# A hybrid layer on one core: the first two weight slots cut finer, two queues for the first loads, and the last product's banks seeded earlier

## The chip, the cores and the metric

The kernel runs on one core of one Trainium2 chip. Its time is the device time of one execution in microseconds. Three runs of the kernel before gave a median of 928.58 us (928.54 to 929.57). The profile is one further execution with its own time of 928.34 us; its span, from the first to the last recorded instruction, is 926.5 us.

TensorE is called PE here, VectorE DVE, ScalarE ACT, GpSimd POOL, and SP is the engine that issues most of the DMAs.

## The reference

One layer over 512 tokens of width 1024, float32: a norm, a mixer of three branches (retention, sliding-window attention, a gated linear recurrence) with sigmoid gates, a cross-attention into 256 memory tokens, and a gated ConvFFN, each added to the residual, and a last norm.

```python
for l in range(DEPTH):                     # DEPTH = 1
    h = rms_norm(x, norm_mix_g[l])
    x = x + hybrid_mixer(h, w_in[l], swa_sinks[l], lb_all[l], hg_norm_g[l], w_branch[l],
                         w_out[l], cos, sin)
    h = rms_norm(x, norm_mem_g[l])
    x = x + mem_xattn(h, rms_norm(mem, mem_norm_g[l]), w_mq[l], w_mkv[l], w_mo[l])
    h = rms_norm(x, norm_ffn_g[l])
    ...
```

`rms_norm` multiplies a token by `rsqrt(mean(x * x) + EPS)` and by a gain per channel. The mixer's first product is `h @ w_in`, cut by columns into the inputs of the branches. The last product is `(silu(a) * u) @ w_down`; behind it stand the residual sum and the last norm.

## The kernel before

**Precision.** Every large product is done in three matmuls of a rounded format: an upper part and a lower part of each operand, as upper x upper, upper x lower, lower x upper. For activations these are `hH` and `hL`, for weights `wH` and `wL`. ACT makes an upper part by a copy, DVE the lower part by subtracting it from the original. A matmul is 128x128 by 128x512.

**Slots.** Weights of the mixer come in slots of 256 columns: slot c uses the buffers `raw`, `wH` and `wL` number c % 2. SP loads `raw` (L432), ACT writes `wH` (the helper `hi`, L1256), DVE writes `wL` (`lo`, L1651), and PE multiplies (`pair_T`, L685): 2 halves of columns x 8 blocks of 128 channels x 3 = 48 matmuls, written transposed, channels on partitions and the 512 tokens along the row. Two PSUM banks take a slot's halves; DVE reads them and multiplies by a row of the tokens' `rstd`, since the norm's factor is left out of h until then (`read_T`). The semaphores are `half_ready` and `lo_ready` (weights split), `h_ready` (a block of h split), `taken` (banks read).

**The start.** x arrives with tokens on partitions, so PE transposes it in 32 blocks of 128x128 (L763): first the 16 of channel blocks 0 to 3 of all four token tiles, later the 16 of blocks 4 to 7. ACT copies each transposed block with its gain into `hH`, DVE makes `hL`. Slot 0's weights come in three parts of channels (0-1, 2-3, 4-7), and PE works on a part when both it and h are there. ACT also squares x by token tile, with a sum along the row, for `rstd`; PE turns `rstd` into a row (`rows_of`, L745) and DVE copies the row out of PSUM before it reads slot 0. DVE computes the angles of the rotary tables in between (`ang`, `whole`), ACT their sines, PE transposes the tables (`wide`, L739).

What an engine does, and in which order, is written out by hand: each engine has its own program, and the engines meet only in semaphores. In DVE's loop the order for slot c is: the split of slot c + 1 (not for c = 0), `job(c)`, the read of slot c. `job(0)` is the copy of the rstd row. So the split of slot 2's weights stands behind `job(0)` and the read of slot 0:

```python
for c in range(N_G0):
    n = Slot(c)
    ...
    if c:
        lo(n + 1, 2048 if c + 1 < N_G0 else 12 * P)
    if c != 5:
        job(c)
```

**The tail.** The last product (`w_down`) ends with 18 late steps (L1216), each in one half of a slot; the last six compute the second 512 columns of token tiles 0 and 1, the last three of them first for tile 0, then for tile 1. PSUM banks 0 and 1 hold that result, and ACT had put the residual into them (`seeds` at step 5). After the last matmul DVE subtracts a stored term `uv` from the bank and writes `otok` (`added`), ACT squares and sums it and takes the root, DVE takes the reciprocal and scales by it and the gain, and two queues store the last halves of tile 1.

## Time and profile before

| what | value |
|---|---|
| median of three runs | 928.58 us |
| profiled execution, its own time | 928.34 us |
| span of the profile | 926.5 us |
| PE busy | 915.9 us (99%), 4494 instructions |
| DVE busy | 628.0 us (68%) |
| ACT busy | 405.2 us (44%) |
| POOL busy | 99.4 us (11%) |
| granted clock of PE | 0.998 of full speed |
| HBM read and written | 159 GB/s over the span |

The 40 slices of the page show PE at nine tenths in all of them but the first (8) and the last (7). The costliest groups are the three forms of the L685 matmul, 784 each, about 306 us each. A matmul row lasts 0.39 us though one starts every 0.23 us: they are pipelined. The chain that ended last runs over PE for 96% of the span.

### The profile page before, as it was taken

The numbers are of one execution on the slowest core, as the hardware profiler recorded it, in microseconds if no ns is written. First come the engines' busy times: TensorE is split into PE (matmuls) and PEld (weight loads), VectorE is DVE, ScalarE is ACT, GpSimd is POOL, SyncE is SP. The second block draws the span as 40 slices with busy tenths as digits, with TensorE's granted clock in tenths as the row PEclk, the third lists the DMA queues.
The fourth block names the chain that finished last, engine by engine and source line by source line (L and its number), as shares of the span: only waits on it lengthen the run. The fifth ranks groups of instructions, "written<-read, shape, count | busy, mean of one in ns | idle before, by whom it ended". The sixth has DMA issues, their size and how long they took to land.

```text
span 926.5 us, 11546 instructions
## 1 busy us (share of the span) xinstructions
PE 915.9 (99%) x4494; PEld 762.9 (82%) x4494; DVE 628.0 (68%) x752; ACT 405.2 (44%) x474; POOL 99.4 (11%) x116
## 2 busy tenths in 40 slices
PE   8999999999999999999999999999999999999997
PEld 6888888888888888888888988888888888888886
DVE  5887555554779466666545658678877677777786
ACT  6464211432365542433433646443333443455684
POOL 0024242300241000000021004100000000000002
PEclk9999999999999999999999999999999999999999
DMA  7558899124798827633324224333355533255563
GB/s 221 180 158 234 209 247 253 46 80 114 171 220 191 215 63 198 159 99 100 118 91 137 69 69 137 91 91 91 91 134 141 132 91 91 91 177 204 175 211 131
DMA packets 137477, 132.48 MB, mean 143 GB/s; under 512 B 6650, under 2 KB 115294, under 8 KB 137182
## 3 DMA queue, kind: packets, MB, share of 16 engines
q1 hardware_dynamic: 127438, 108.62, 39.2%
q0 software_dynamic: 9856, 23.07, 11.3%
q8 instruction: 26, 0.43, 0.2%
q10 hardware_dynamic: 144, 0.26, 0.1%
q14 instruction: 13, 0.11, 0.0%
HBM read 122.23 MB, written 25.17 MB: 159 GB/s over the span
## 4 chain that ended last, share of the span: by engine, by line
PE 96%; DVE 2%; DMA 0%; ACT 0%; SPq 0%; issue 0%; DVEq 0%
PE ps L685 74%; PE ps L1204 6%; PE ps L1216 5%; PE ps L1080 5%; PE ps L739 1%; PE ps L823 1%; PE ps L1108 1%; DVE wL L1651 0%; PE ps L921 0%; PE ps L887 0%; DMA invf<-in_consts 0%; PE ps L847 0%; PE ps L942 0%; PE ps L907 0%; DVE cu L1658 0%; PE ps L849 0%
## 5 line engine op out<-in xcount | busy, mean ns | idle before, releaser
L685 PE MATMUL ps<-hH,wH 128*128 128x512 f32 x784 | 307.9, 393 | 2.5 <-DVE wL L1651 2.1
L685 PE MATMUL ps<-hH,wL 128*128 128x512 f32 x784 | 305.2, 389 | 0.0
L685 PE MATMUL ps<-hL,wH 128*128 128x512 f32 x784 | 305.2, 389 | 0.0
L1651 DVE TENSOR_TENSOR wL<-raw,wH 128x2048 fp32r<-128x2048 f32 (+3 forms) x119 | 209.5, 1768 | 63.3 <-ACT wH L1256 63.0
L1256 ACT ACTIVATE wH<-raw 128x2048 fp32r<-128x2048 f32 (+3 forms) x119 | 175.9, 1487 | 143.3 <-PE ps L685 132.1
L685 PEld LDWEIGHTS ps<-hH,wH 128*128 128x128 f32 x784 | 147.2, 188 | 34.9 <-DVE wL L1651 3.5
L685 PEld LDWEIGHTS ps<-hH,wL 128*128 128x128 f32 x784 | 147.2, 188 | 31.0
L685 PEld LDWEIGHTS ps<-hL,wH 128*128 128x128 f32 x784 | 147.2, 188 | 29.9 <-issue 0.2
L1256 ACT ACTIVATE ca<-za,par 128x512 f32<-128x512 f32 x22 | 18.0, 816 | 100.4 <-DVE za L1651 100.4
L1658 DVE SCALAR_TENSOR_TENSOR ca<-za,par,ca 128x512 f32<-128x512 f32 x44 | 33.1, 752 | 25.6 <-ACT ca L1256 23.4
L1658 DVE SCALAR_TENSOR_TENSOR cu<-zu,par,cu 128x512 f32<-128x512 f32 x44 | 33.1, 752 | 25.4 <-ACT cu L1256 23.3
L1256 ACT ACTIVATE gate<-gate 128x512 f32<-128x512 f32 x24 | 15.2, 632 | 72.8 <-DVE gate L1651 72.7
L674 POOL TENSOR_TENSOR g<-otok,gainF 128x512 f32<-128x512 f32 x1 | 5.4, 5419 | 328.3 <-DVE otok L1651 328.3
L1651 DVE TENSOR_TENSOR sL<-pair,sH 128x512 fp32r<-128x512 f32 (+2 forms) x29 | 25.0, 863 | 16.2 <-ACT sH L1256 16.2
L1204 PE MATMUL ps<-wH,sH 128*128 128x512 f32 x88 | 34.4, 390 | 0.2 <-DVE wL L1651 0.2
L1256 ACT ACTIVATE sH<-pair 128x512 fp32r<-128x512 f32 (+2 forms) x29 | 22.2, 765 | 28.1 <-PE ps L1204 19.0
L1204 PE MATMUL ps<-wH,sL 128*128 128x512 f32 x88 | 34.2, 389 | 0.0
L1204 PE MATMUL ps<-wL,sH 128*128 128x512 f32 x88 | 34.2, 389 | 0.0
L1256 ACT ACT_TABLE_LOAD x26 | 33.4, 1283 | 1.2 <-PEq L2411 0.8
L1256 ACT ACTIVATE ca<-ca 128x512 f32<-128x512 f32 x22 | 13.9, 633 | 36.8 <-DVE ca L1658 36.8
L635 POOL DMA_DIRECT2D t<-in_w_down x11 | 6.3, 569 | 192.6 <-PE ps L685 125.7
L1256 ACT ACTIVATE hH<-xT,par 128x512 fp32r<-128x512 f32 x16 | 11.6, 722 | 33.9 <-DVE xT L1651 33.9
(319 smaller groups left out, 1460.7 us busy)
## 6 DMA issues: line engine op xcount, KB each, us to landing
raw<-in_w_in SPq DMA_DIRECT2D x57, 512.0 KB, 4.9
raw<-in_w_up SPq DMA_DIRECT2D x44, 512.0 KB, 4.6
t<-in_w_down POOLq DMA_DIRECT2D x66, 256.0 KB, 5.8
raw<-t SPq DMA_DIRECT2D x11, 768.0 KB, 4.7
raw<-in_w_branch SPq DMA_DIRECT2D x24, 256.0 KB, 4.9
t<-t POOLq DMA_DIRECT2D x22, 256.0 KB, 9.9
raw<-in_w_down SPq DMA_DIRECT2D x10, 512.0 KB, 4.1
raw<-in_w_out SPq DMA_DIRECT2D x8, 512.0 KB, 4.4
```

The source lines that it names most:

```text
L635: pool.dma_start(t123[a, 1, :], w_down[0, a, 0:S]).then_inc(t_sum, 16)
L674: pool.tensor_tensor(g11[:, :], otok[:, 1, 0:S], gainF[:, 0:S], ALU.mult).then_inc(d_gain, 1)
L685: last = pe.matmul(out_ap, a, b, start=start and k + m == 0, stop=stop and m == 2 and k == len(terms) - 1)
L739: last = pe.transpose(out_ap, in_ap, ident[0:k, 0:k])
L823: last = pe.matmul(o, a, b, start=True, stop=True)
L1080: last = pe.matmul(ps[:, 2 * n.s + e, :], x, y[:, k, :], start=k + m == 0, stop=k == KD - 1 and m == 2)
L1108: last = pe.matmul(ps[:, h ^ 2, :], mV[:, m, P * h:P * h + P], mPT[h % 2][:, m, :], start=m == 0, stop=m == MT - 1)
L1204: last = pe.matmul(ps[:, b + t, :], x, w[s][:, S * q:S * q + S], start=i == 0 and j == 0, stop=i == NP - 1 and j == 2, skip_group_check=True)
L1216: last = pe.matmul(ps[:, b + t, :], x, w[s][:, f], start=False, stop=m % NG == NG - 1 and j == 2, skip_group_check=True)
L1256: q.sig(act.activation(out_ap, in_ap, fn, **kw), sem)
L1651: q.sig(dve.tensor_tensor(out_ap, a, b, op), sem)
L1658: q.sig(dve.scalar_tensor_tensor(out_ap, a, s, b, op0, op1), sem)
```

## The change

**Start.** The four quarters of the channels (blocks 2j and 2j + 1) take the place of the two halves. x is loaded by quarters, in two DMAs of two token tiles each; slot 0's weights are split in four quarters; PE transposes a quarter of x between the first and the second column half of the quarter before. ACT issues six of the first DMAs (identity, gains, two weight quarters, positions, frequencies) on its own queue. DVE's angle steps stand between the quarters.

**Second slot.** Its weights are split in two halves. The squares of x come after both on ACT. PE does its first 24 matmuls, then the parameters' transposes, 12 matmuls, then `job(0)` (the row of `rstd`), then the last 12. Until now parameters and row stood before the slot. The table transposes move from behind slot 1 to behind slot 2; the constant tables are loaded after slot 3's weights.

**Tail.** DVE, at step 5, writes the residual less `uv` into banks 0 and 1. ACT squares the bank itself and DVE scales from it; the subtraction behind the last matmul is gone.

```diff
+            def x_quarter(j):
+                c = slice(2 * P * j, 2 * P * j + 2 * P)
+                for a in range(2):
+                    t = slice(2 * a, 2 * a + 2)
+                    sp.dma_start(xtok[:, t, c], xsrc[:, t, c]).then_inc(x_in[2 * j + a], 16)
+
+            x_quarter(0)
+            x_quarter(1)
+            sp.dma_start(*first_slot(2)).then_inc(first_in[2], 16)
+            x_quarter(2)
+            sp.dma_start(*first_slot(3)).then_inc(g_row, 16)
+            x_quarter(3)
+            v = raw[1][:, :].rearrange("p (k c) -> p k c", k=KD)
+            for k, w, sem in ((0, 4, mem_in), (4, 2, raw_in[1]), (6, 2, raw_in[1])):
+                sp.dma_start(v[:, k:k + w, :], win[:, k:k + w, PAIRS[1]:PAIRS[1] + 256]).then_inc(sem, 16)
...
+                if c == 3:
+                    tables()
...
 
-            def x_half(half):
+            def x_quarter(j):
+                if j >= 2:
+                    pe.wait_ge(h_ready, 2 * j - 2)
                 for t in range(NT):
-                    pe.wait_ge(x_in[NT * half + t], 16)
-                    for k in range(4 * half, 4 * half + 4):
+                    if t % 2 == 0:
+                        pe.wait_ge(x_in[2 * j + t // 2], 16)
+                    for k in range(2 * j, 2 * j + 2):
                         last = x_tile(t, k)
                         if t == NT - 1:
                             last.then_inc(xT_out, 1)
-                    if half == 0 and t == 0:
+                    if j == 0 and t == 0:
 
                         pe.wait_ge(mix_in, 16)
                         transposes([(ps[:, 2, R_GAIN:R_GAIN + KD], rows_gain[:, 0, :])], mix_T)
-                    if half == 0 and t == 1:
-                        pe.wait_ge(pos_f, 1)
-                        transposes([(ps[:, 2, 256:256 + NT], rows_posf[:, :])], pos_T)
 
...
-                elif n == 1:
+                elif n == 2:
...
-                    if c:
+                    if c > 1:
                         pair_T(n, hH, hL)
                     else:
                         vh, vl = weights(n, KD, 256)
 
-                        def piece(e, ks, done=None, ready=None):
+                        def piece(e, ks, ready=None):
                             cc = slice(P * e, P * e + P)
-                            product(ps[:, e, :], [(vh[:, k, cc], vl[:, k, cc], hH[:, k, :], hL[:, k, :]) for k in ks],
-                                    done, ks[0] == 0, ks[-1] == KD - 1, ready, ks[0] + 1)
-
-                        for part in range(2):
-                            pe.wait_ge(half_ready, part + 1)
-                            piece(0, range(2 * part, 2 * part + 2), None, h_ready)
-                        piece(1, range(0, 2))
-                        second_half()
-                        piece(1, range(2, 4))
-                        pe.wait_ge(lo_ready, 1)
-                        piece(0, range(4, KD), first_done, h_ready)
-                        piece(1, range(4, KD), slot_done)
-                        parameters()
+                            product(ps[:, 2 * n.s + e, :],
+                                    [(vh[:, k, cc], vl[:, k, cc], hH[:, k, :], hL[:, k, :]) for k in ks],
+                                    (first_done, slot_done)[e] if ks[-1] == KD - 1 else None,
+                                    ks[0] == 0, ks[-1] == KD - 1, ready, ks[0] + 1)
+
+                        if c == 0:
+                            for j in range(4):
+                                if j == 3:
+                                    pe.wait_ge(lo_ready, 1)
+                                else:
+                                    pe.wait_ge(half_ready, j + 1)
+                                piece(0, range(2 * j, 2 * j + 2), h_ready)
+                                if j < 3:
+                                    x_quarter(j + 1)
+                                piece(1, range(2 * j, 2 * j + 2))
+                        else:
+                            pe.wait_ge(half_ready, 4)
+                            piece(0, range(4))
+                            piece(1, range(4))
+                            parameters()
+                            pe.wait_ge(lo_ready, 2)
+                            piece(0, range(4, KD))
+                            job(0)
+                            piece(1, range(4, KD))
                 else:
                     pair_T(n, hH, hL)
-                job(c)
+                if c >= 2:
+                    job(c)
...
+            act.dma_start(ident[:, :], consts[:, K_ID:K_ID + P]).then_inc(ident_in, 16)
+            act.dma_start(rows_gain[:, 0, :], norm_mix_g[0].rearrange("(k p) -> k p", p=P)).then_inc(mix_in, 16)
+            act.dma_start(*first_slot(0)).then_inc(first_in[0], 16)
+            act.dma_start(rows_pos[:, :], positions[0].rearrange("(t p) -> t p", p=P)).then_inc(pos_in, 16)
+            act.dma_start(*first_slot(1)).then_inc(first_in[1], 16)
+            act.dma_start(invf[:, :], consts[:, K_INV:K_INV + 32]).then_inc(inv_in, 16)
             act.wait_ge(set_up, 1)
             do(eps[:, 1:2], eps[:, 0:1], ACT.Copy)
             act.wait_ge(mix_par, 1)
-            h_upper(0)
-            first_hi(0)
-            h_upper(1)
-            first_hi(1)
-            h_upper(2)
-            h_upper(3)
-            for t in range(NT - 1):
+            for j in range(4):
+                h_upper(2 * j)
+                first_hi(j)
+                h_upper(2 * j + 1)
+            for k in range(2):
+                if k:
+                    act.wait_ge(raw_in[1], Slot(1).loads())
+                else:
+                    act.wait_ge(mem_in, 16)
+                f = slice(1024 * k, 1024 * k + 1024)
+                do(wH[1][:, f], raw[1][:, f], ACT.Copy, hi_ready if k else first_half)
+            for t in range(NT):
                 square_sum(t)
-            first_hi(2)
-            for k in range(4, KD):
-                h_upper(k)
-            square_sum(NT - 1)
-            hi(Slot(1))
             q.settle()
             do(rstd[:, NT:2 * NT], ssq[:, 0:NT], ACT.Sqrt, std_ready, scale=1.0 / D, bias=eps[:, 0:1])
+            hi(Slot(2))
             act.wait_ge(fn_arg, 1)
-            do(lbt[:, 1, :], lbt[:, 0, :], ACT.Exp, fn_out)
-            act.wait_ge(fn_arg, 2)
             do(trig[:, 0], ang[:, :, :], ACT.Sin, fn_out, scale=0.5)
             do(trig[:, 1], ang[:, :, :], ACT.Sin, fn_out)
+            act.wait_ge(fn_arg, 2)
+            do(lbt[:, 1, :], lbt[:, 0, :], ACT.Exp, fn_out)
...
             for t in range(2):
-                act.wait_ge(d_out, 10 + t)
-                square_of(t, 1, None)
+                act.wait_ge(d_sum, 9 + t)
+                square_of(t, 1, None, ps[:, t, :])
...
+            def first_lo(j):
+                if j == 3:
                     dve.wait_ge(hi_ready, 1)
                 else:
-                    dve.wait_ge(first_half, part + 1)
-                f = (slice(0, 512), slice(512, 1024), slice(1024, 2048))[part]
+                    dve.wait_ge(first_half, j + 1)
+                f = slice(512 * j, 512 * j + 512)
                 tt(wL[0][:, f], raw[0][:, f], wH[0][:, f].bitcast(F32), ALU.subtract,
-                   lo_ready if part == 2 else half_ready)
+                   lo_ready if j == 3 else half_ready)
...
-            h_lower(0)
-            first_lo(0)
-            h_lower(1)
-            first_lo(1)
-            h_lower(2)
-            h_lower(3)
-            turns_off(1)
+            for j in range(4):
+                h_lower(2 * j)
+                first_lo(j)
+                h_lower(2 * j + 1)
+                if j == 0:
+                    angles()
+                elif j < 3:
+                    turns_off(j - 1)
+            second_lo(0)
+            second_lo(1)
             turns_off(2)
...
+            dve.wait_ge(std_ready, 1)
+            q.sig(dve.reciprocal(rstd[:, 0:NT], rstd[:, NT:2 * NT]), rstd_ready)
+            dve.wait_ge(par_T, 1)
+            copy(par[:, 0:G_MIX], ps[:, 7, 0:G_MIX])
+            copy(par[:, G_MIX + KD:R_ALL], ps[:, 7, G_MIX + KD:R_ALL], par_ready)
...
                 elif n == 4:
+                    constants()
...
+                elif m == 5:
+                    dve.wait_ge(x2_in, 528)
+                    dve.wait_ge(d_out, 3)
+                    for t in range(2):
+                        tt(as_res(ps[:, t, :]), res_half(t, 1), as_res(uv[:, t, :]), ALU.subtract, d_seed)
...
+            def last_half(t, sem):
+                stt(otok[:, t, S:D], ps[:, t, :], ostat[:, t, 3:4], gainF[:, S:D], ALU.mult, ALU.mult, sem)
+
             for t in range(2):
-                dve.wait_ge(d_sum, 9 + t)
-                added(t, 0, uv, 1, ALU.subtract, d_out)
                 dve.wait_ge(o_sum, 7 + t)
                 inverse(t)
                 q.settle()
-                scaled(t, S * t, D, o_fin)
+                last_half(t, o_fin if t else None)
+                if t == 0:
+                    scaled(t, 0, S, o_fin)
```

A transfer borrows the semaphores `mem_in` and `g_row` once each, so their later waits count 16 more; those lines are not shown. `angles()` is what stood ahead of `h_lower(0)` before, without its first `turns_off`.

On PE at the start, before: the first product, the second half's transposes (`xtok`), and the next products. `ps` is PSUM, `restart` the warm-up, `x_in` the loads of x.

```order
L768 MATMUL ps<-restart 128x128 x3
L685 MATMUL ps<-hH,wH_53 128x512 [waits h_ready,half_ready]
...
L685 MATMUL ps<-hH,wH_53 128x512 [waits h_ready,half_ready]
...
L763 MATMUL ps<-ident,xtok 128x128 [waits x_in4,h_ready]
...
L685 MATMUL ps<-hH,wH_53 128x512
...
L685 MATMUL ps<-hH,wH_53 128x512 [waits h_ready,lo_ready]
```

The same place after the change:

```order
L771 MATMUL ps<-restart 128x128 x3
L688 MATMUL ps<-hH,wH_53 128x512 [waits h_ready,half_ready]
...
L766 MATMUL ps<-ident,xtok 128x128 [waits x_in2]
...
L688 MATMUL ps<-hH,wH_53 128x512
...
L688 MATMUL ps<-hH,wH_53 128x512 [waits h_ready,half_ready]
...
L766 MATMUL ps<-ident,xtok 128x128 [waits x_in4,h_ready]
...
L688 MATMUL ps<-hH,wH_53 128x512
...
L688 MATMUL ps<-hH,wH_53 128x512 [waits h_ready,half_ready]
...
L766 MATMUL ps<-ident,xtok 128x128 [waits x_in6,h_ready]
```

Eight transposes now stand in front of the first product instead of sixteen, and each further eight stand between six matmuls and six.

On PE from the end of slot 0 to the start of slot 2, before (`rows_conv` are parameters, `rstd` the row, `wide` the tables; `wH_54` is slot 1, `wH_53` slot 0 or 2):

```order
L739 MATMUL ps<-ident,rows_conv 128x44 [waits par_in]
L739 MATMUL ps<-ident,rows_conv 128x44 x3
L739 MATMUL ps<-ident,rows_gain 128x8 x4
L739 MATMUL ps<-ident,rows_hg 128x4 x2
L745 MATMUL ps<-ident,rstd 128x128 [waits rstd_ready]
L745 MATMUL ps<-ident,rstd 128x128 x3
L685 MATMUL ps<-hH,wH_54 128x512 [waits lo_ready]
...
L739 MATMUL ps<-ident,wide 128x128 [waits wide_ready]
L739 MATMUL ps<-ident,wide 128x128 x7
L685 MATMUL ps<-hH,wH_53 128x512 [waits taken,lo_ready]
```

And after:

```order
L688 MATMUL ps<-hH,wH_54 128x512 [waits half_ready]
...
L742 MATMUL ps<-ident,rows_conv 128x44 [waits par_in]
L742 MATMUL ps<-ident,rows_conv 128x44 x3
L742 MATMUL ps<-ident,rows_gain 128x8 x4
L742 MATMUL ps<-ident,rows_hg 128x4 x2
L688 MATMUL ps<-hH,wH_54 128x512 [waits lo_ready]
...
L748 MATMUL ps<-ident,rstd 128x128 [waits rstd_ready]
L748 MATMUL ps<-ident,rstd 128x128 x3
...
L688 MATMUL ps<-hH,wH_53 128x512 [waits taken,lo_ready]
```

Parameters and row moved from before slot 1 into it, the row to 12 matmuls before its end, and the tables out of this stretch.

On DVE around the copy of the row, before (`wL_55` is slot 2's lower part, `ang` angles, `hgF` the read of slot 0):

```order
L1734 RECIPROCAL rstd<-rstd 128x4 [waits std_ready]
L1661 COPY par<-ps 128x176 [waits par_T]
L1661 COPY par<-ps 128x40
L1651 TENSOR_TENSOR lbt<-par 128x4 [waits par_ready]
L1658 SCALAR_TENSOR_TENSOR ang<-whole_98,ang 128x128 [waits fn_arg]
...
L1752 RECIPROCAL lbt<-lbt 128x4 [waits fn_out]
...
L1661 COPY rstd_row<-ps 128x512 [waits row_out]
L1651 TENSOR_TENSOR hgF<-ps,rstd_row 128x512 [waits first_done,dve_step]
L1651 TENSOR_TENSOR hgF<-ps,rstd_row 128x512 [waits slot_done]
L1651 TENSOR_TENSOR wL_55<-raw_51,wH_53 128x2048 [waits hi_ready]
```

And after:

```order
L1671 TENSOR_SCALAR ang<-ang 128x128 [waits dve_step]
L1765 RECIPROCAL rstd<-rstd 128x4 [waits std_ready]
L1678 COPY par<-ps 128x176 [waits par_T]
L1678 COPY par<-ps 128x40
L1668 TENSOR_TENSOR lbt<-par 128x4 [waits par_ready]
L1678 COPY rstd_row<-ps 128x512 [waits row_out]
L1668 TENSOR_TENSOR hgF<-ps,rstd_row 128x512 [waits first_done,dve_step]
L1668 TENSOR_TENSOR hgF<-ps,rstd_row 128x512 [waits slot_done]
L1668 TENSOR_TENSOR wL_55<-raw_51,wH_53 128x2048 [waits hi_ready]
```

The order of the row's copy, the two reads and the split is the same; what stands before them changed, and the row they wait for is issued later.

## Rows read from the trace of the kernel before

**Rows 1.** The page, part 1: busy time of each engine.

```profile
PE 915.9 (99%) x4494; PEld 762.9 (82%) x4494; DVE 628.0 (68%) x752; ACT 405.2 (44%) x474; POOL 99.4 (11%) x116
```

**Rows 2.** Waits of PE over the span: total, times, longest us.

```profile
PE ps L685 <- DVE wL L1651: 2.1, 1, 2.1
...
PE ps L685 <- DVE hL L1658: 0.3, 1, 0.3
```

**Rows 3.** Timeline of the start: start us, us, what, idle time before.

```profile
4.54 1.06 PE L763 MATMUL ps<-ident,xtok 128*128 128x128 f32 x4
...
7.30 0.66 PE L763 MATMUL ps<-ident,xtok 128*128 128x128 f32 x4 [0.22 <-DMA xtok<-in_x]
...
7.74 0.69 ACT L1256 ACTIVATE hH<-ps,par 128x512 fp32r<-128x512 f32 x1 [5.48 <-PE ps L763]
...
9.35 0.74 DVE L1658 SCALAR_TENSOR_TENSOR hL<-ps,par,hH 128x512 fp32r<-128x512 f32 x1
...
10.75 0.50 PE L685 MATMUL ps<-hH,wH 128*128 128x512 f32 x1 [2.12 <-DVE wL L1651]
```

**Rows 4.** Timeline around the second sixteen transposes.

```profile
15.60 1.91 PE L763 MATMUL ps<-ident,xtok 128*128 128x128 f32 x16
...
17.21 2.42 ACT L1256 ACTIVATE hH<-ps,par 128x512 fp32r<-128x512 f32 x4 [1.22 <-PE ps L763]
...
17.26 0.48 PE L685 MATMUL ps<-hH,wH 128*128 128x512 f32 x1
...
17.93 2.73 DVE L1658 SCALAR_TENSOR_TENSOR hL<-ps,par,hH 128x512 fp32r<-128x512 f32 x4 [0.69 <-ACT hH L1256]
```

**Rows 5.** Timeline of PE around slot 1.

```profile
24.51 0.44 PE L739 MATMUL ps<-ident,rows_conv 44*128 44x44 f32 x4
...
25.34 1.16 PE L745 MATMUL ps<-ident,rstd 128*128 128x128 f32 x8
...
26.25 0.48 PE L685 MATMUL ps<-hH,wH 128*128 128x512 f32 x1
...
37.26 1.03 PE L739 MATMUL ps<-ident,wide 128*128 128x128 f32 x8
...
38.05 0.48 PE L685 MATMUL ps<-hH,wH 128*128 128x512 f32 x1
```

**Rows 6.** Timeline of DVE beside slot 1.

```profile
31.21 0.68 DVE L1661 COPY rstd_row<-ps 128x512 f32<-128x512 f32 x1
...
33.13 2.28 DVE L1651 TENSOR_TENSOR wL<-raw,wH 128x2048 fp32r<-128x2048 f32 x1
```

**Rows 7.** Stretches of 1 us: busy by engine, clock, DMA share, GB/s.

```profile
3.00:4.00 1.00, 1.00 (x7) 1.00 (x6) 0.00 (x0) 0.00 (x0) 0.00 (x0) 1.00 0.57 113
...
4.00:5.00 1.00, 1.00 (x7) 1.00 (x7) 0.00 (x0) 0.00 (x0) 0.00 (x0) 1.00 1.01 369
```

**Rows 8.** Timeline of the tail.

```profile
920.66 0.69 DVE L1651 TENSOR_TENSOR otok<-ps,uv 128x512 f32<-128x512 f32 x1
...
921.38 0.63 ACT L1256 ACTIVATE junk<-otok 128x512 f32<-128x512 f32 x1 [2.35 <-DVE otok L1651]
...
922.66 0.75 DVE L1658 SCALAR_TENSOR_TENSOR otok<-otok,ostat,gainF 128x512 f32<-128x512 f32 x1
```

**Rows 9.** Groups of the first 40 us: busy us, mean ns.

```profile
L1256 ACT ACTIVATE hH<-ps,par 128x512 fp32r<-128x512 f32 x8 | 5.0, 683 | 6.7 <-PE ps L763 6.7
...
L1256 ACT ACTIVATE wH<-raw 128x512 fp32r<-128x512 f32 x2 | 1.2, 623 | 0.2 <-DMA raw<-in_w_in 0.2
...
L1256 ACT ACTIVATE junk<-xtok 128x1024 f32<-128x1024 f32 x4 | 4.2, 1060 | 0.3
```

**Rows 10.** Timeline of DVE in the last product.

```profile
885.54 0.69 DVE L1651 TENSOR_TENSOR wL<-raw,wH 128x512 fp32r<-128x512 f32 x1
...
887.88 1.29 DVE L1651 TENSOR_TENSOR otok<-res,otok 128x512 f32<-128x512 f32 x2
```

**Rows 11.** One stretch of the last product, columns as in rows 7.

```profile
880.00:910.00 30.00, 30.00 (x133) 24.50 (x132) 27.59 (x38) 24.00 (x40) 0.00 (x0) 1.00 0.58 196
```

164 lines of the change are left out of this document (75 added, 89 removed).

## The prediction

> **What bounds the kernel now.** I read the page first, then the waits of PE, then the timeline of the first 50 us and of the last 10 us, because the change edits only these ends. PE is busy for 99% of the span [rows 1], so every microsecond that PE waits is lost and work hidden under PE costs nothing. Its waits after the warm-up are one of 2.1 us, for the lower half of the first weights, and one of 0.3 us, for the lower half of h [rows 2]. So two stretches are open: the start up to 10.75 us, and the tail behind the last matmul, where DVE, ACT, DVE and a store follow each other.
>
> The start reads so [rows 3]: PE transposes x from 4.54 us; the last token tile's group starts at 7.30, and ACT writes the first hH at 7.74. DVE could take it 0.72 us later, as it does at 17.93 [rows 4], but comes only at 9.35, since it works on the rotary angles until then; then hL, wL, and PE starts its first product at 10.75. From there each engine's order counts: a slot of 48 matmuls takes 37.26 - 26.25 = 11.01 us, 0.229 each [rows 5].
>
> I compare one point in both kernels, the start of slot 3. Before, slot 2 starts at 38.05 after the table transposes, so slot 3 starts at 38.05 + 11.01 = 49.05. From there to the last stage both kernels issue the same PE work.
>
> **Part 1, the first product.** Only 8 transposes stand before it and no angles. PE starts them at 4.54 as before (the warm-up matmuls are kept). The first four took 1.06 us, so the last token tile starts after two at that speed (0.5), the gain transposes (0.15) and four at 0.17 (0.7): 5.9 us. From that group's start to hH is at most 7.74 - 7.30 = 0.44, of which I take 0.35: hH at 6.2. hH to hL is 17.93 - 17.21 = 0.72 [rows 4]; hL to the first matmul is 10.75 - 9.35 = 1.40 [rows 3]. The first product starts at 6.2 + 0.72 + 1.40 = 8.3, which is 2.4 us earlier. Bounds: 8.0 if all four transposes already run at the later speed; 9.5 if x lands no sooner than now.
>
> **Part 2, quarters.** The loop is now: 8 transposes, six matmuls of the previous quarter's second half, wait, six matmuls of the new quarter. Sixteen transposes take 17.26 - 15.60 = 1.66 [rows 4], 0.104 each, so the cover on PE is 0.83 + 6 x 0.229 = 2.2, about 2.3 with the restart. What it must cover runs in series: the quarter's seventh transpose is the one that frees hH, 6 x 0.104 + (17.21 - 15.60 - 12 x 0.104) = 0.98 after the first started; then 0.72 to hL and 1.40 through hL and wL to PE: 3.10. ACT's weight copy hides, since hH and wH end 1.3 after hH's start and DVE reaches wL 1.4 after it. So each quarter waits 3.10 - 2.3 = 0.8 us, three times 2.4. Before, the second half of slot 0 had no such wait: its weights were split before its transposes. Slot 0 is: 1.5 (first six) + 3 x 3.10 + 2 x 1.5 + 2.8 (last twelve) = 16.6, so it ends at 24.9. Before it ended at 24.4. The early start is spent inside slot 0. Bounds for the wait: 0 if ACT and DVE overlap more than these rows show; 1.4 each if the angle steps, which DVE now runs between quarters, are still running (about 1.2 us of them in a gap of 4.6 - 2.0 us, so I expect none).
>
> **Part 3, slot 1 and what stands behind it.** The squares of x (four of 1.06 us plus their readouts, 5 us) go behind the halves of slot 1 on ACT. From hH of quarter 3 on, ACT has 1.7 of copies, 2 for slot 1's halves, 4 x 1.06 for the squares [rows 9] with readouts 5.0, and 1.6 for the root: 10.3 us; PE wants rstd only 14 us after it, so they cost nothing, and the time of the angles on DVE (4 us) is hidden by the same room. But the row of rstd, which PE formed before slot 1, is now formed after 36 of its 48 matmuls. Parameters take 25.34 - 24.51 = 0.83 and the row 26.25 - 25.34 = 0.91 on PE, done 1.16 after its start [rows 5]. The row is out at 24.9 + 5.5 + 0.83 + 2.75 + 1.16 = 35.1. On DVE the row's copy, the two reads of slot 0 and the split of slot 2's weights stand in that order and last 33.13 + 2.28 - 31.21 = 4.20 [rows 6]; slot 2 waits for the last of them. So slot 2 starts at 35.1 + 4.20 + 0.1 = 39.4, while PE is free at 24.9 + 5.5 + 0.83 + 2.75 + 0.91 + 2.75 = 37.6: a new wait of 1.8 us. Before, DVE copied the row at 31.2 and the split was done 2.6 us before PE came. Bounds: 0 to 2.1, the latter with DVE late on its way to the copy. Then 11.0 for slot 2 and 0.79 for the table transposes (38.05 - 37.26) now behind it: slot 3 starts at 51.2, which is 2.2 us later than before.
>
> What queues behind that wait: DVE's split of slot 3, ACT's sigmoid and the forget-gate work. Slot 3's split ends at about 45 and PE wants it at 51, so they recover. The tables on the sync queue move behind slot 3's load; masks and the rest are wanted slots later.
>
> **Part 4, two queues.** The scalar queue takes the identity, gains, the first two weight quarters, positions and frequencies. One queue already moved 369 GB/s with a share of 1.01 in the fifth microsecond [rows 7]; quarter 0 of x, with what runs beside it, is 0.84 MB, 2.3 us from 1.9 on, and with about 1 us until its semaphore (PE's wait for the last tile ended at 7.3, a microsecond after as many bytes had moved) lands at about 5.2, when PE wants it. I cost this at nothing, between -0.3 and +1.2 (x as late as now).
>
> The Trainium skill, "DMA: Bandwidth & Descriptors", section "Issuing engines are not separate DMA queues", says that all issuers' transfers interleave on the same 16 engines and that a second issuer only saves issue time. The trace agrees, with that share of 1.01 on one queue. By it the second queue gains no bandwidth and makes x wait for weights; without it x's first half megabyte would land 0.9 us sooner, which the warm-up on PE hides anyway.
>
> **Part 5, the tail.** The last token tile's residual is seeded before the last products, so DVE's subtraction behind the last matmul goes: ACT's square started 921.38 - 920.66 = 0.72 after it [rows 8]. The square now reads PSUM. A 128x512 ACT copy from PSUM took 0.683 mean, from SBUF 0.623 [rows 9]: +0.06. The final scaling reads PSUM too; the same form from PSUM took 0.74 [rows 3] and from SBUF 0.75 [rows 8]: 0. So the tail gives 0.72 - 0.06 = 0.66, between 0.6 and 0.8. The seeds move from ACT to DVE, two of 0.65 [rows 10], where DVE is 92% busy (27.59 of 30 us) [rows 11]. At that place the splits run ahead: the sixth step's ends at 885.54 + 0.69 = 886.2 [rows 10], and PE, which needs 66 x 0.227 = 15.0 for each six steps and ended at 920.6, comes to it at 920.6 - 30.0 - 1.4 = 889.2; the next have at least 2.3 us. So 1.3 us more is hidden; with that cover gone it would cost up to 1.3.
>
> The Trainium skill, "VectorE: DVE Perf Modes", section "The TRN2 errata — SBUF-src ops pay a fixed extra latency per instruction", gives ScalarE 224 + N cycles from SBUF and 172 + N from PSUM, an estimate of 0.04 us less from PSUM. The rows here show 0.06 more, with a scale operand, and I keep the row. By the rule the tail would give 0.76.
>
> **Sum.** Against the profiled execution (span 926.5, its own time 928.34): start +2.2, tail -0.66, that is +1.5. The median of the runs, 928.58, is 0.24 over the profiled one. 928.58 + 1.5 = 930.1. A measurement of this kernel tells some 0.2%, 1.86 us, from no change: below 926.72 is faster, above 930.44 slower. The forecast is a small loss just inside "same".
>
> **Rivals.**
> *PE alone bounds the start.* If DVE and ACT keep pace, the 2.4 us in the quarters and the 1.8 us before slot 2 vanish: 930.1 - 4.2 = 925.9, faster. For it: DVE's work per quarter, 2.0 + 1.2, is less than PE's 3.6. Against it: the steps are in series, each with its row. It decides once both waits sum to under 0.8 us.
> *Only one wait is real.* The serial rows overlap in the quarters but slot 2 waits: 930.1 - 2.4 = 927.7; or the reverse, 928.3. Same.
> *Transfers bound the start.* Today PE waits for x until 7.30. If x's quarter, now interleaved with two weight quarters, lands no sooner, the first product starts at 9.5, everything shifts 1.2 us: 931.3, slower. For it: the fourth microsecond moved only 113 GB/s [rows 7]. Against: a third less data has to land first. It decides from 0.4 us of delay.
> *Seeds collide.* If DVE's fuller order holds up PE in the last product, up to 1.3 us more: 931.4, slower. The slack of 2.3 us speaks against it.
>
> **How the numbers follow.** Forecast with both waits, 929.2 to 931.0: 0.50. One wait: 0.18. PE alone: 0.13. Transfers: 0.13. Seeds or another loss: 0.06. Faster takes the PE-alone case less its upper edge, 0.12. Same takes 0.6 of the forecast (its part under 930.44) and the one-wait case, 0.49. Slower takes the rest, 0.39. The range 927.3 to 931.8 leaves out PE-alone and a few hundredths above.
>
> **What would show it.** Right: the first L685 product near 8.3; three PE waits of about 0.8 on DVE's wL before 21 us; slot 0 ending near 24.9; one PE wait near 1.8 before slot 2 at about 39.4; slot 3 at 51.2; 0.66 less from last matmul to end; no PE wait in the last 40 us. Wrong: waits in the quarters under 0.4, a PE wait on x, or a first product after 9.

## The result, and the profile after

The changed kernel takes 932.34 us in the median of 8 runs (931.4 to 933.48), beside 928.59 before (8 runs, 928.1 to 930.14). The ratio is 1.0036, 95% interval 1.0027 to 1.0044: slower by 3.35 us. The forecast was 930.1, with a range up to 931.8. The sign was the forecast's, the size was not.

PE waits after the change, in total, times and longest us; before there was one wait of 2.1 and one of 0.3 [rows 2], and one of 0.2 for x [rows 3]:

```profile
PE ps L688 <- DVE wL L1668: 3.8, 5, 1.5
PE ps L771 <- DVE eps L1691: 1.8, 1, 1.8
PE ps L1216 <- DVE wL L1668: 0.2, 1, 0.2
```

The first row holds three waits of 0.67 inside slot 0, the one before slot 2, and 0.26 before the first product. All of these were forecast, and they come to 3.8 us where the old head waited 2.7 (2.12, 0.34 and 0.22). That is 1.1 us of the loss; the rest is in no row of waits, since PE counts as busy in it. It shows when the start is read as a timeline (start us, us, what, idle time before; one copy, to be held against [rows 3] and [rows 5]):

```profile
5.30 1.54 PE L766 MATMUL ps<-ident,xtok 128*128 128x128 f32 x6
...
6.55 0.21 DVE L1678 CAST rows_posf<-rows_pos 4x128 f32<-4x128 int32 x1 [0.98 <-DMA rows_pos<-in_positions]
...
7.52 0.75 DVE L1675 SCALAR_TENSOR_TENSOR hL<-ps,par,hH 128x512 fp32r<-128x512 f32 x1 [0.76 <-ACT hH L1268]
...
8.93 0.80 PE L688 MATMUL ps<-hH,wH 128*128 128x512 f32 x1 [0.26 <-DVE wL L1668]
...
9.52 0.63 PE L688 MATMUL ps<-hL,wH 128*128 128x512 f32 x1
...
11.36 1.04 PE L766 MATMUL ps<-ident,xtok 128*128 128x128 f32 x8
...
12.16 0.47 PE L688 MATMUL ps<-hH,wH 128*128 128x512 f32 x1
...
14.46 0.50 PE L688 MATMUL ps<-hH,wH 128*128 128x512 f32 x1 [0.67 <-DVE wL L1668]
...
35.70 1.05 PE L748 MATMUL ps<-ident,rstd 128*128 128x128 f32 x8
```

The six transposes from 5.30 take 0.25 us each, where the kernel before had reached 0.17 by 5.7 us. The first product starts at 8.93 instead of 8.3. Its matmuls follow each other after 0.59 and then 0.43 us, up to 10.8; the six take 11.36 - 8.93 = 2.43 us instead of 1.5. From 12.16 on they stand 0.23 us apart. From there the forecast's pitch holds: 14.46 - 11.36 = 3.10 us from one group of transposes to the next product, as written.

Slot 0 ends at 26.48 (forecast 24.9), the rstd row's copy starts at 36.79 (35.1), slot 2 at 41.05 (39.4), slot 3 at 52.87 (51.2):

```profile
36.79 0.69 DVE L1678 COPY rstd_row<-ps 128x512 f32<-128x512 f32 x1 [3.19 <-PE ps L748]
...
38.72 2.28 DVE L1668 TENSOR_TENSOR wL<-raw,wH 128x2048 fp32r<-128x2048 f32 x1
...
41.05 0.50 PE L688 MATMUL ps<-hH,wH 128*128 128x512 f32 x1 [1.55 <-DVE wL L1668]
...
52.08 1.03 PE L742 MATMUL ps<-ident,wide 128*128 128x128 f32 x8
...
52.87 0.48 PE L688 MATMUL ps<-hH,wH 128*128 128x512 f32 x1
```

From the end of the first six matmuls to slot 3 the forecast had 51.2 - 9.8 = 41.4 us, and the trace has 52.87 - 11.36 = 41.51. So the whole excess of the start, 1.6 us, lies before 11.36.

The tail, after the last matmul (compare [rows 8]):

```profile
924.24 0.39 PE L1228 MATMUL ps<-wH,sL 128*128 128x512 f32 x1
...
924.66 0.60 ACT L1268 ACTIVATE junk<-ps 128x512 f32<-128x512 f32 x1 [2.38 <-PE ps L1228]
...
925.91 0.75 DVE L1675 SCALAR_TENSOR_TENSOR otok<-ps,ostat,gainF 128x512 f32<-128x512 f32 x1
...
926.69 0.33 SPq L619 DMA_DIRECT2D out<-otok  x1
```

The last matmul ends at 924.24 + 0.39 = 924.63, and the last store is issued 926.69 - 924.63 = 2.06 us later. The same two before, and the start of slot 3 before:

```profile
49.02 0.39 PE L685 MATMUL ps<-hH,wH 128*128 128x512 f32 x1
...
920.23 0.39 PE L1216 MATMUL ps<-wH,sL 128*128 128x512 f32 x1
...
923.44 0.33 SPq L616 DMA_DIRECT2D out<-otok  x1
```

That was 923.44 - 920.62 = 2.82 us: 0.76 gained, forecast 0.66. The square from PSUM takes 0.60 us, less than the 0.63 from the buffer.

The sum for this execution, whose own time is 931.67: start of slot 3 +3.85 (52.87 - 49.02), from there to the last matmul +0.16, tail -0.76, that is +3.25 of the 3.33 between the two profiled executions.

### The profile page after: what moved, and what is told of

The parts are those of the page before. It is cut to its first block, busy times and chain, and to the rows that moved or that the text cites. A ratio compares the mean times of both kernels' runs of the same rounds, so it can differ in the third digit from the quotient of the medians.

```text
span 929.9 us, 11558 instructions
## 1 busy us (share of the span) xinstructions
PE 918.7 (99%) x4494; PEld 764.3 (82%) x4494; DVE 628.1 (68%) x755; ACT 404.6 (44%) x474; POOL 99.6 (11%) x116
## 4 chain that ended last, share of the span: by engine, by line
PE 96%; DVE 3%; ACT 1%; issue 0%; DVEq 0%; ACTq 0%
PE ps L688 73%; PE ps L1216 6%; PE ps L1228 5%; PE ps L1092 5%; PE ps L742 1%; PE ps L823 1%; DVE wL L1668 1%; PE ps L1120 1%; PE ps L766 0%; PE ps L921 0%; PE ps L887 0%; PE ps L847 0%; PE ps L942 0%; PE ps L907 0%; DVE cu L1675 0%; DVE hL L1675 0%
```

## The experiments

Ratios are to the kernel before in the same session; 0.001 is 0.93 us. Where two kernels are compared in microseconds, I take the difference of their ratios.

**1. The tail alone.**

```diff
-                elif m == 5:            # ACT
-                    act.wait_ge(d_out, 3)
-                    seeds((0, 1), 1, 0)
+                elif m == 5:            # DVE
+                    dve.wait_ge(x2_in, 528)
+                    dve.wait_ge(d_out, 3)
+                    for t in range(2):
+                        tt(as_res(ps[:, t, :]), res_half(t, 1), as_res(uv[:, t, :]), ALU.subtract, d_seed)
...
-                added(t, 0, uv, 1, ALU.subtract, d_out)
```

> The kernel before with the tail of the change alone (last token tile's banks seeded by DVE, square and last scaling read from PSUM). My theory: the subtraction behind the last matmul goes, its square comes 0.04 us after the matmul: 0.72 us less from last matmul to last store, no new PE wait, so 927.9 against 928.6. Rival (seeds on DVE collide with the splits): a PE wait on wL or sL in the last 40 us, and 0 to 1.3 us slower than that.

Measured: 928.43, ratio 0.9995 (0.9986 to 1.0004). The timed difference, 0.5 us less, is inside its noise, so the expected 0.7 is not shown by the times; the trace shows it. Matmul, square and store of the tail alone:

```profile
920.49 0.39 PE L1216 MATMUL ps<-wH,sL 128*128 128x512 f32 x1
...
920.91 0.60 ACT L1256 ACTIVATE junk<-ps 128x512 f32<-128x512 f32 x1 [2.38 <-PE ps L1216]
...
922.94 0.33 SPq L616 DMA_DIRECT2D out<-otok  x1
```

The store comes 922.94 - 920.88 = 2.06 us after the last matmul, as in the full change, and PE has no new wait. The rival with the seeds falls.

**2. The head alone** (the changed kernel with the hunks of experiment 1 taken back).

> The changed kernel with the tail of before. Theory (the loss is all in the first 53 us: 1.55 us before slot 2, the rest in slot 0): start of slot 3 at 52.9, 4.0 to 4.4 us slower than before, some 932.9. Rival (part of the loss comes from DVE's fuller order at the end): under 3.5 us slower, and the last stretch shorter than in the changed kernel.

Measured: 933.37, ratio 1.0049 (1.0036 to 1.0063), so 4.6 us. I expected 4.0 to 4.4. The loss is the head's. (With the tail's 0.5 taken off, 4.1 would be left for the whole change, which measured 3.35; five runs, timed apart from the changed kernel, don't settle the difference.) Its trace holds an execution of another kind, which mattered later:

```profile
5.30 0.93 PE L766 MATMUL ps<-ident,xtok 128*128 128x128 f32 x6
...
7.72 0.21 DVE L1680 CAST rows_posf<-rows_pos 4x128 f32<-4x128 int32 x1 [2.15 <-DMA rows_pos<-in_positions]
...
7.99 0.22 PE L742 MATMUL ps<-ident,rows_posf 4*128 4x4 f32 x1 [1.77 <-DVE rows_posf L1680]
...
8.14 1.01 PE L771 MATMUL ps<-restart 128*128 128x128 f32 x6
...
9.38 0.79 PE L688 MATMUL ps<-hH,wH 128*128 128x512 f32 x1 [0.22 <-DVE wL L1670]
...
12.10 1.12 PE L766 MATMUL ps<-ident,xtok 128*128 128x128 f32 x8
```

Here the transposes had been fast (0.93 us for six). Then the positions landed at 7.7 us, DVE stood for them, and PE stood for DVE until 7.99. The six warm-up turns right behind that wait were still fast (1.01 us). Only then the speed was lost: the granted clock went from 1.00 to 0.50, from 2.4 to 1.2 GHz, at about 8.86 us, while PE was at these turns, and came back at about 12.3. The first product, 9.38 to 12.10, ran at 0.43 us a matmul. One microsecond of it (busy time by engine, clock, DMA share, GB/s):

```profile
9.00:10.00 1.00, 0.78 (x3) 0.53 (x3) 1.00 (x3) 0.00 (x0) 0.00 (x0) 0.50 1.11 351
```

The 1.8 us of idle time came before the fall; that they caused it is likely, not shown. In the trace of the kernel before PE was idle for 2.1 us ahead of its first product and started it fast [rows 2, 3].

**3. Slot 2's split ahead of the row on DVE.**

```diff
-                if c:
+                if c == 0:
+                    lo(Slot(2))
+                elif c > 1:
                     lo(n + 1, 2048 if c + 1 < N_G0 else 12 * P)
                 if c != 5:
                     job(c)
```

> The changed kernel with DVE's split of slot 2's weights ahead of its copy of the rstd row and the reads of slot 0. Theory (PE's 1.55 us before slot 2 is the order on DVE alone): the split runs at 33.6 to 35.9 in DVE's idle time, reads of slot 0 end at 38.7, before PE comes at 39.4; the wait is gone and the time falls by 1.5 us to 930.8. Rival (the row itself is too late, whatever the order): a wait of 0.7 us or more on the reads of slot 0 remains, time 931.6 or more.

Measured: 930.87, ratio 1.0024 (1.0015 to 1.0033). DVE and the end of slot 2:

```profile
32.10 2.29 DVE L1668 TENSOR_TENSOR wL<-raw,wH 128x2048 fp32r<-128x2048 f32 x1
...
35.37 0.69 DVE L1678 COPY rstd_row<-ps 128x512 f32<-128x512 f32 x1 [0.99 <-PE ps L748]
...
48.81 1.03 PE L742 MATMUL ps<-ident,wide 128*128 128x128 f32 x8
```

The split runs in DVE's idle time, and the PE wait is gone. The time is the expected 930.8. The traces show 1.85 us less between the same two points: 48.81 - 9.93 here, from the first product's end to slot 2's end, against 50.60 - 9.87 in the trace "look2" below. The medians show 1.1 to 1.5. The rival (the row itself is too late) falls.

**4. The weights of quarters 1 to 3 ahead of h.**

```diff
-                h_lower(2 * j)
-                first_lo(j)
+                if j:
+                    first_lo(j)
+                h_lower(2 * j)
+                if j == 0:
+                    first_lo(j)
                 h_lower(2 * j + 1)
```

(and the same for ACT's two operations)

> The changed kernel with, for quarters 1 to 3, ACT's and DVE's work on the weights ahead of their work on h instead of between its two tiles. Theory (the 0.67 us before each quarter is the serial chain transposes, hH, hL, wL): the link wL leaves the chain, 0.98 + 0.72 + 0.72 = 2.4 us stand against a cover of 2.4, waits fall to under 0.1 each, 1.8 to 2.0 us less, 930.4. Rival (weights come late or ACT is the bound): waits stay over 0.4 each, gain under 0.8 us.

Measured: 930.63, ratio 1.0020 (1.0011 to 1.0029). The three waits of 0.67 became:

```profile
PE ps L688 <- DVE hL L1678: 0.5, 3, 0.2
```

0.17 each, where I expected under 0.1; 930.4 was expected. The serial chain was the cause, and its third link can be taken out.

**5. Both.**

> The changed kernel with both edits: slot 2's split ahead of the rstd row on DVE, and the weights of quarters 1 to 3 ahead of h. Theory (both waits are real and add up): 1.5 and 1.7 us less than the changed kernel, 929.2, about the same as before; no PE wait over 0.3 us after the first product. Rival (one wait takes the other's place, because the row comes only 0.72 us after the split could end): 930.4.

Measured: 929.50, ratio 1.0008 (0.9998 to 1.0017); expected 929.2. In the trace slot 2 ends 47.72 - 10.45 = 37.27 us after the first product's end; "look3" below has 51.19 - 10.45 = 40.74. That is 3.47 less, the sum of 1.85 and 1.62 (experiment 4: 49.57 - 10.45 = 39.12). So the two waits are independent and add up. With both gone the kernel is still no faster than before, although its tail is shorter.

**6. What delays or slows the first product: positions, one queue, warm-up.**

```diff
@@ e6_positions @@
-            pe.wait_ge(pos_f, 1)
-            transposes([(ps[:, 2, 256:256 + NT], rows_posf[:, :])], pos_T)
             busy(3)
...
                                 piece(0, range(2 * j, 2 * j + 2), h_ready)
+                                if j == 0:
+                                    pe.wait_ge(pos_f, 1)
+                                    transposes([(ps[:, 2, 256:256 + NT], rows_posf[:, :])], pos_T)
@@ e7_one_queue: the six act.dma_start of the head go to sync @@
+            x_quarter(0, (0,))
+            sp.dma_start(ident[:, :], ...)
+            sp.dma_start(rows_gain[:, 0, :], ...)
+            sp.dma_start(rows_pos[:, :], ...)
+            x_quarter(0, (1,))
+            sp.dma_start(*first_slot(0)).then_inc(first_in[0], 16)
@@ e8_turns @@
-            busy(6)
+            busy(10)
```

> The changed kernel with the positions taken out of the way of the first product: DVE's cast behind the first weights' split and PE's transposes of them behind the first six matmuls. In the traces so far the positions landed at 6.5 to 7.7 us, and where PE stood 1.8 us for them the first product ran at 0.43 us a matmul for 2.7 us. Theory (DVE's wait for that transfer, and PE's idle time after it, delay the start and keep the clock low in some executions): no PE wait between 5 and 8 us, 0.3 to 1 us less, 931.7. Rival (the clock rises when it rises, and positions cost nothing at the median): 932.3.

> The changed kernel with all first transfers on the sync queue, in the order x, identity, gains, positions, x, first weights quarter. Theory (the second queue saves issue time and puts the positions behind 256 KB of weights): positions land before 6 us, x's second half 1 us later; the two about cancel, 932.0 to 932.8. Rival (two queues bring the start that the change needs): first product 0.7 us later or more, 933 or above.

> The changed kernel with 10 instead of 6 warm-up turns on PE, which puts its first transposes 1.96 us later (4 turns of 0.49). Theory (the first product starts before PE runs at its upper level, so that an early start is paid with slow matmuls): only part of the 1.96 us is lost, 0.5 to 1.3 us slower than the changed kernel, 933.2, and all matmuls of the first product at 0.23 us. Rival (speed of the first product does not depend on when it starts): 1.9 us slower, 934.2.

Measured: positions 931.36, ratio 1.0028 (1.0017 to 1.0039); one queue 930.69, ratio 1.0018 (1.0009 to 1.0027); turns 931.76, ratio 1.0029 (1.0017 to 1.0042). The first is within the noise of the changed kernel's 1.0036. The second is 1.7 us better, a miss of my expectation by more than its interval. The third was to lose 0.5 to 1.3 us by my theory and lost nothing. (The changed kernel was timed apart from these three, so these are differences of ratios, each to its own runs of the kernel before.) Positions in the one-queue kernel, and its first product:

```profile
5.49 0.20 DVE L1679 CAST rows_posf<-rows_pos 4x128 f32<-4x128 int32 x1
...
9.12 0.80 PE L695 MATMUL ps<-hH,wH 128*128 128x512 f32 x1 [0.32 <-DVE wL L1669]
```

The positions are there at 5.5 us. Even so this execution (931.75, one of its slowest) ran its first product at the slow pace. With four more turns:

```profile
5.58 0.38 PE L766 MATMUL ps<-ident,xtok 128*128 128x128 f32 x2
...
6.05 0.87 PE L766 MATMUL ps<-ident,xtok 128*128 128x128 f32 x6
...
9.12 0.50 PE L688 MATMUL ps<-hH,wH 128*128 128x512 f32 x1 [1.18 <-DVE wL L1668]
```

The transposes start 1.05 us later, not 1.96, since the turns had sped up, and six of them then take 0.87 us instead of 1.54. The first product starts 0.19 later than in the changed kernel's trace and takes 1.5 us.

**7. The changed kernel again, and four single executions of it.** These are the same program as the changed kernel.

> The changed kernel once more, unchanged, beside the three others on one chip. Theory (the moment at which PE's matmuls go from 0.43 to 0.23 us is not set by the program; it lay between 5 and 12 us in traces with the same work before it): again 3 to 4 us over before with a spread of 2 us; the trace may show another moment than 11.1 us, and then a slot 2 that starts as much earlier. Rival (in this kernel the late rise is systematic, because its first transposes are fewer): the trace shows the rise after 10 us again.

> The changed kernel, one look. If the late rise makes the upper level, an execution over 932.3 shows matmuls of 0.43 us in the first product and one under 931.1 none; its slot 2 ends over 52.0 us. If late positions do, it shows a PE wait of over 1 us for them at 6 to 8 us.

> The changed kernel, one look. If the difference between its two levels lies after the first 50 us, slot 2 ends at the same time (51.2 us, 0.2 either way) whatever the execution's own time.

> The changed kernel, a third look, with the same three readings: matmuls of 0.43 us in the first product, a PE wait for the positions, or neither and the time spent later.

> The changed kernel, a fourth look, with the same three readings: matmuls of 0.43 us in the first product, a PE wait for the positions, or neither and the time spent later.

Again: 932.63 median of 8 (930.69 to 933.37), ratio 1.0033 (1.0022 to 1.0044). Six traces of one program, each with its own time (all in us):

```
trace        own time  first product  its end  slot 2 ends  own time - its end
look2         930.19       8.37         9.87      50.60         920.32
look1         930.45       8.65        10.15      50.84         920.30
again         930.74       8.94        10.43      51.16         920.31
look3         930.96       8.94        10.45      51.19         920.51
the result's  931.67       8.93        11.36      52.08         920.31
look4         931.86       9.09        11.60      52.30         920.26
```

The last column is constant to 0.25 us. What differs between executions of this kernel is the moment at which the first six matmuls are done, and nothing after it. So the rise after 10 us is not systematic, and the expectation with "look2", that slot 2 ends at 51.2 whatever the time, was wrong: it ends at 50.60 to 52.30. The two ends of the table as rows, look2 and then look4:

```profile
5.30 0.88 PE L766 MATMUL ps<-ident,xtok 128*128 128x128 f32 x6
...
6.80 0.22 PE L742 MATMUL ps<-ident,rows_posf 4*128 4x4 f32 x1 [0.63 <-DVE rows_posf L1678]
...
8.37 0.50 PE L688 MATMUL ps<-hH,wH 128*128 128x512 f32 x1 [0.48 <-DVE wL L1668]
...
9.87 1.03 PE L766 MATMUL ps<-ident,xtok 128*128 128x128 f32 x8
...
50.60 1.03 PE L742 MATMUL ps<-ident,wide 128*128 128x128 f32 x8
```

```profile
5.31 1.54 PE L766 MATMUL ps<-ident,xtok 128*128 128x128 f32 x6
...
6.97 1.65 PE L771 MATMUL ps<-restart 128*128 128x128 f32 x6
...
9.09 0.80 PE L688 MATMUL ps<-hH,wH 128*128 128x512 f32 x1 [0.47 <-DVE wL L1668]
...
11.60 0.60 PE L766 MATMUL ps<-ident,xtok 128*128 128x128 f32 x4
...
52.30 1.03 PE L742 MATMUL ps<-ident,wide 128*128 128x128 f32 x8
```

Look2 had its speed by 5.3 us: six transposes in 0.88. Look4 had it only after the first product: transposes at 0.25, turns 1.65 us instead of 0.94, product 2.5 us instead of 1.5. Up to the transposes at 5.3 us PE did the same work in both. Look2 is the execution that the forecast describes: first product 8.37 (forecast 8.3), slot 2 at 39.58 (39.4), time 930.19 (930.1).

Of the 16 runs of the changed kernel that are behind the two medians, ten lie between 932.2 and 933.5, above every trace of the table. The trace of experiment 2 lies there too, once its longer tail (0.76) is taken off: 932.5. With positions moved 1 run of 7 lies above 932.2, with one queue none of 11 (the highest is 932.16), with ten turns none of 6. Their traces show no idle time between the transposes and the turns. I infer that the upper level is what experiment 2's trace shows: PE fast, idle, and slow again. The mean granted clock of the runs speaks for it: 0.998 or 0.997 in eight of the ten, 0.999 or 1.000 in the six lower runs, and 0.998 in experiment 2's trace. Two things speak for caution: the highest two runs of the ten have 0.999, and the end of an execution, where the clock reads 0.50 too, can lower the mean by 0.002 by itself. No trace of the unchanged program caught the upper level, so this is likely and not shown, and it would be why the median (932.3) lies 0.7 above the profiled execution.

The kernel before has two such levels as well. Its 81 runs beside the experiments fall into 44 from 928.07 to 928.94 and 37 from 929.18 to 930.50, medians 928.55 and 929.73. The mean clock is 0.997 in 20 of the upper ones and in none of the lower. Its trace, with the own time of 928.34, is of the lower level; the upper one was never traced.

**8. Versions that might win.** All three kernels have the new tail.

```diff
@@ e12b_angles_later: the kernel before with the new tail, and DVE's angles moved @@
-            dve.wait_ge(pos_T, 1)
-            ...
-            turns_off(0)
             h_lower(0)
             first_lo(0)
             h_lower(1)
             first_lo(1)
             h_lower(2)
             h_lower(3)
+            dve.wait_ge(pos_T, 1)
+            ...
+            turns_off(0)
@@ e10b_one_queue: experiments 3 and 4 and the one queue of 6; e11b_turns: that with busy(8) @@
```

> Both edits of the orders (slot 2's split first, weights of quarters 1 to 3 first) and all first transfers on the sync queue, with the change's tail. Theory (the one queue's gain of 1.6 us at the median comes from the positions, landed by 5.5 us, and adds to the 2.8 of the two edits): 3.35 - 2.8 - 1.6 = 1.0 us faster than before. Rival (the gains overlap, the first product is late either way): as without the one queue, 0.7 us slower than before.

> The same as the kernel with both orders and one queue, with 8 instead of 6 warm-up turns on PE. Theory (longer work of PE ahead of the first product lets more executions run it at 0.23 us a matmul, and the transposes' delay of up to 1 us is hidden because they then run faster): 0.3 to 0.8 us faster than with 6 turns. Rival: the transposes are on the path and the time is 0.5 to 1 us longer.

> The kernel before with the change's tail and, of its head, only the angles on DVE moved behind the first four tiles of h. Theory (in the kernel before only DVE's angles stand between 7.74 and the first product): hL at 8.5 instead of 9.35, first product 0.6 to 0.9 us earlier, at 10.0, and later waits grow by 0.3 at most: 0.4 to 0.8 us faster than the tail alone. Rival (the weights' transfer, landed at 8.6, or the order on ACT takes the wait's place): under 0.3 us.

Measured: one queue with both orders 927.45, ratio 0.9984 (0.9975 to 0.9993); with 8 turns 927.43, ratio 0.9982 (0.9973 to 0.9991), a spread of 0.9 us instead of 1.85 and no better median, so that expectation missed; angles later 927.90, ratio 0.9983 (0.9974 to 0.9992). By their ratios the three beat the kernel before by 1.5 to 1.7 us (by their medians by 1.0 to 1.5), and the changed one, which ran beside them at 1.0033, by 4.6 to 4.7; they don't differ from each other. The first was expected 1.0 us faster than before and is 1.5. Its trace gains nothing by the one queue: own time less end of the first product is 927.27 - 10.52 = 916.75, and 927.28 - 10.45 = 916.83 in experiment 5's. The plainest of them is the old head with one block of DVE's program moved behind four operations:

```profile
8.29 0.69 ACT L1256 ACTIVATE hH<-ps,par 128x512 fp32r<-128x512 f32 x1 [6.03 <-PE ps L763]
...
9.08 0.75 DVE L1656 SCALAR_TENSOR_TENSOR hL<-ps,par,hH 128x512 fp32r<-128x512 f32 x1 [2.96 <-ACT hH L1256]
...
10.49 0.50 PE L685 MATMUL ps<-hH,wH 128*128 128x512 f32 x1 [1.31 <-DVE wL L1649]
```

In this execution the transposes were slow (hH at 8.29, 7.74 before), and the first product still starts 0.26 earlier than before, since DVE no longer does the angles first. But the gain does not last. The angles now stand ahead of the hL of blocks 4 to 7, and PE waits for that, 0.64 us at 19.26; its waits on hL in all:

```profile
PE ps L685 <- DVE hL L1656: 1.0, 2, 0.6
```

With the tail alone it was 0.4, and slot 1's products ended at 37.50 there and at 37.65 here. So the trace shows no gain over the tail alone, where 0.4 to 0.8 us was expected, though the ratios differ by 1.1. Beside the lower level of the 30 runs of the kernel before that were timed with it (median 928.56) this kernel is 0.7 us faster, which is the tail's 0.76. What is left is that none of its 11 runs (927.41 to 928.09) lies a level higher, while 14 of those 30 did. PE's idle time ahead of its first product is 1.3 us instead of 2.1, which may be why; no run tests it.

## Why the prediction was wrong

**The step that failed** is the pace of PE at the start: Part 1, "PE starts them at 4.54 as before ... the last token tile starts after two at that speed (0.5), the gain transposes (0.15) and four at 0.17 (0.7)", and the term "1.5 (first six)" in Part 2. I took the moment at which PE got fast, 5.6 us in one trace, for a property of the program. Thirteen traces with the same work on PE up to 5.1 us (this kernel's six, and those of seven experiments) put it between about 5.5 and 7.7 us in ten and at about 11 in three (the result's, "look4", the one queue). In the profiled execution it cost 0.6 us in the transposes (first product at 8.93, not 8.3) and 0.9 in the first product (2.43, not 1.5), 1.5 together. It brings 930.1 to 931.6, and that execution's own time is 931.67; the other 0.7 us to the median is the level above it, whose cause stays open as far as no trace of this program shows it. The warning I had was that the runs of the kernel before spread by 1 us.

Does the kernel before pay too? In its two traced heads (its own and the tail alone) PE stood 2.1 us before its first product at 10.75 [rows 3] and 11.01 and was fast when it started. There slow transposes cost 0.26 us, where a product that starts at 8.4 can spend its gain on matmuls at half pace. Ten warm-up turns, which delay the transposes by a microsecond, cost nothing, probably for the same reason. But the upper level of 37 of its 81 runs says that it often pays in the other way, 1.2 us. The forecast compared with one trace of the lower level and had no term for the level in either kernel.

The profile's granted clock shows one kind of slow stretch and not the other. In experiment 2, where PE had been fast, it reads 0.50 over the slow product. Before PE has first got fast it reads 1.00 all the same. The changed kernel at the slow pace, then look2 in the same stretch (busy time by engine, clock, DMA share, GB/s):

```profile
9.00:10.00 1.00, 1.00 (x3) 0.81 (x4) 0.96 (x5) 0.00 (x0) 0.00 (x0) 1.00 1.09 373
```

```profile
9.00:10.00 1.00, 1.00 (x7) 0.79 (x6) 0.04 (x1) 0.00 (x0) 0.00 (x0) 1.00 1.11 362
```

Both read 1.00, which is the clock of 2.4 GHz, with 3 matmuls in one and 7 in the other. 512 columns in 0.43 us is one a cycle at 1.2 GHz; at 0.23 us it is near one a cycle at 2.4. The Trainium skill, "TensorE: Matmul & The Clock Gate", Part 1, says that the number of slow matmuls at a kernel's start varies from run to run, because the gate's phase is free at the start. The six traces agree as to the varying number; the phase itself is in no trace. The same place advises against fitting a model to the ramp, since it is small beside a span; here 1.5 us was nearly half of the measured effect of 3.35 and decided between a range held and missed.

**Part 4, two queues, "I cost this at nothing".** The x transfers came when PE wanted them, as costed; PE waits on x in no trace of the new head. What I didn't follow was the positions. They moved behind 256 KB of weights on the scalar queue. In the six traces of the changed kernel and those of experiments 2 to 5, DVE took them at 6.37 us or later (7.72 at worst) and waited 0.8 to 2.2 us for them; in the one-queue kernel it took them at 5.49 without a wait. DVE's cast of them stands ahead of hL. But only in experiment 2's trace did they hold hL up; in the others DVE then waited for hH, 0.22 us or more, and in look4 and experiment 2 ACT waited 0.26 and 0.62 us for the first weights as well. I had counted what each transfer brings PE and not who stands for the smallest of them. The one-queue kernel is 1.7 us better by the ratios. That the positions are why is not shown: with the positions alone moved out of the way the gain was 0.7 us, inside the noise. The rival "transfers bound the start" came out at 931.3 and named x, and x was not it.

**The rest of Part 2, and Part 3, were right.** Pitch 3.10, three waits of 0.67 (forecast 0.8), a wait of 1.55 before slot 2 (1.8), 41.05 - 36.79 = 4.26 us from the row's copy to the slot (4.20). Experiment 3 removed the wait before slot 2 and experiment 4 cut the others to 0.17 by the order alone, so the causes are shown. The rival "PE alone bounds the start" needed both edits and only then comes near: 1.0008.

**Part 5 was right in kind and 0.10 short.** The square from PSUM is 0.03 us quicker than from the buffer, not 0.06 slower. I had priced it from an operation with a scale operand. The rule of the Trainium skill, "VectorE: DVE Perf Modes", section "The TRN2 errata — SBUF-src ops pay a fixed extra latency per instruction", 0.04 less by the prediction's estimate, was the better price: the tail gave the 0.76 that the prediction worked out from it. The seeds cost PE nothing, as said.

**The range** ended at 931.8, since it added only one late transfer to the forecast. Half pace at the start gives 931.6, which it held by accident; the upper level, 932.2 to 933.5, belonged in it too.

## What to carry to other kernels

An early first product is worth less than it looks while PE has not reached its pace: price the first microseconds of PE at both paces, and look at several executions of the start before trusting one. Sort the timed runs of both kernels into levels, too, since a median moves with the share of each; a change can win by leaving the upper one, as the angles moved later seem to. When work is cut into smaller pieces to start sooner, each piece pays the serial chain of its producers; put the operand that doesn't depend on the latest input ahead of the one that does. And follow every small transfer to the engine that reads it in order, since it can hold up all that stands behind, as the positions did in experiment 2.

## What the runs showed of the hardware that was not expected

- PE's change from 0.43 to 0.23 us a matmul came between about 5.5 and 7.7 us in ten traces and at about 11 in three, with the same work up to 5.1 us. The granted clock read 1.00 in all of them up to that first change, so also while PE ran at half pace.
- In one trace (experiment 2) PE was fast at 5.3 to 6.2 us, idle until 7.99, still fast for six warm-up turns, and slow from 9.38 to 12.1, with a granted clock of 0.50 from about 8.86 to 12.3. In the traces of the kernel before and of experiment 1, with 2.1 us idle ahead of the first product, it did not fall. What decides stays open.
- The kernel before runs at two levels 1.2 us apart (37 of 81 runs at the upper), with a mean granted clock of 0.997 only at the upper one.
- ACT's square of 128x512 takes 0.60 us from PSUM and 0.63 from the buffer.
